# Reordering the last three steps of the FFN stages in a 10-stage transformer kernel on one Trainium2 core

## The chip, the cores and the metric

The kernel runs on one core of one Trainium2 chip, as one launch. The metric is the device time of one execution in microseconds (us). PE is the matmul engine (PEld its weight loads), DVE the vector engine, ACT the scalar engine, POOL the GpSimd engine, SP the engine that issues most DMAs here. Engines run apart from each other and meet at semaphores, which the kernel sets and waits for by hand.

## What is computed

Four transformer layers over 256 tokens of width 1024, in float32. In the reference, each FFN of the first two layers, and each of the last two, is

```python
def conv_ffn(h, w_in, conv_w, conv_b, w_out):
    z = causal_dwconv(h @ w_in, conv_w, conv_b)
    u, g = jnp.split(z, 2, axis=-1)
    return (jax.nn.gelu(g) * u) @ w_out
...
    h = rms_norm_2(x, g_ffn)
    a = depthwise_conv(h @ w_ffn_gate, conv_w, conv_b)
    x = x + (jax.nn.gelu(a) * (h @ w_ffn_up)) @ w_ffn_down

    e = rms_norm_2(pe @ w_ple_proj, g_ple)
    g = jax.nn.sigmoid(rms_norm_2(x, g_ple_in) @ w_ple_gate)
    return x + g * e
```

with D_FF = 2816. The last three lines are a gated embedding that follows each of the last two FFNs. The other stages are a pooling and attention mixer, a recurrent mixer, and two hybrid mixers with three attentions each. One of these attentions subtracts two softmaxes with a weight `lam` per layer, which is made of exponentials of two dot products of length 64.

## The kernel before

**Stages.** The ten stages are `pa`, `ffn0`, `rg`, `ffn1`, `hy0`, `hf0`, `ple0`, `hy1`, `hf1`, `ple1`. `ffn0` and `ffn1` are the causal FFNs, in which both halves of the first product go through a convolution. `hf0` and `hf1` are the others, in which only the gate half does. Activations live transposed, with the feature on the partition: x, h and so on are 8 tiles of 128 x 256 tokens.

**Weights as units.** All weights lie in HBM as 239 units of 128 x 2048 float32 (1 MB), in the order in which they are used. SP loads unit n into one of two `raw` slots once unit n - 2 has been taken from it (semaphore `lo_done`, in a loop of two loads at L359 to L363). ACT then rounds the unit to fp32r, `w_hi` (L385), and DVE takes the rest, `w_lo` (L794). There are three slots of these, so ACT waits until PE has finished unit n - 3 (`w_used`). In the code of both engines the call `after(n)` stands for this work on unit n + 3, and its place in the instruction order is set by hand.

**Products.** Each product is three matmuls (`three`, L1350 to L1352): hi by hi, hi by lo, lo by hi. Every unit of an FFN is 48 matmuls of 256 columns. The activations have such parts too: `h_hi` and `h_lo` for the normed input, `y_hi` and `y_lo` for the product that goes into the second matmul. ACT writes `y_hi` (L471), POOL writes `y_lo` (L1283, semaphore `ffy`).

**An FFN stage** has 11 steps of 256 features. Step s has two first products, a(s) into PSUM bank 4 and b(s) into bank 5, and then comes the second product of the step before, out(s-1), which adds to banks 0 to 3. So PE's order is a0 b0, a1 b1 out0, a2 b2 out1, ..., a10 b10 out9, out10, which are units 0 to 32 of the stage. In a causal stage, step s goes on like this after its products: DVE scales bank 4 by the row norm (L847), ACT makes the first tap (L446), and DVE adds the other two taps (L875; then semaphore `cvu`). The same happens for bank 5 (L456, L875; then `cvg`). ACT then takes the gelu (L461), DVE multiplies (L915; `ymul`), and ACT and POOL write `y_hi` and `y_lo`. In `hf` stages only bank 4 has taps, and the multiplication reads bank 5 directly. PE may write a(s+1) when the taps of bank 4 are done, and b(s+1) when those of bank 5 (or the multiplication) are done. There is one slot for y. Thus ACT writes `y_hi` of step s only when out(s-1) has been read by PE:

```python
                    act.wait_ge(sems["ymul"], done(1))
                    if s0:
                        act.wait_ge(sems["w_used"], plus(u + 3, i, 6))
                    nc.scalar.activation(pair(y_hi[:, 0], 0), pair(qk, 3), ACT.Copy).then_inc(sems["yhi"], 1)
```

Steps 3 to 8 are a hardware loop of two steps; 0 to 2, 9 and 10 are written out. In steps for which `parts_late` holds (all of `hf`, and step 10 of the causal stages) ACT and DVE do the work on later units behind, and not ahead of, the taps. The second slot of y, `y_hi[:, 1]`, holds the parts of the embedding through an `hf` stage. Its product (`ple`, `onto`) follows out10 directly.

**Between stages.** When a bank of out10 is complete, DVE adds it to x (L858), ACT and DVE write the parts of the next h, ACT squares x (L411), DVE sums the squares, and PE sums over the partitions (L1394). In `hy`, DVE also computes `lam` (L1163 to L1170) with an exponential on ACT (L680), once per layer, and ahead of `hy0` it works out position tables (`geometry`, L1115).

Of the kernel before, what the change touches and what calls it, by code (L numbers as in the profile page):

```python
# [21 lines left out]
ALU = mybir.AluOpType  # L22
# [20 lines left out]
LOOPED = 6  # L43
RG_STEPS = 5
# [40 lines left out]
def build(nc, W, XT, CON, CON0, VEC, PW, RW, PE_T, POSR, POSC, LAM, OUT, stages=STAGES):  # L85
# [4 lines left out]
    with ExitStack() as ctx:  # L90
# [22 lines left out]
        y_lo = sb("y_lo", [P, 2, 2, S], F32R)  # L113
        con = sb("con", [P, con_w])
# [8 lines left out]
        hr_t = sb("hr_t", [P, S])  # L123
        hr = hr_t[0:16, :]
# [10 lines left out]
        posr = sb("posr", [P, S], I32)  # L135
# [208 lines left out]
        @block.sync  # L344
        def _(sp):

            sp.dma_start(vec[:], VEC).then_inc(sems["vec_in"], 16)
            sp.dma_start(x[:], XT).then_inc(sems["x_in"], 16)
            sp.dma_start(raw[:, 0], W[first]).then_inc(raw_in[0], 16)
            sp.dma_start(con[:], CON).then_inc(sems["con_in"], 16)  # L350
            sp.dma_start(raw[:, 1], W[first + 1]).then_inc(raw_in[1], 16)
            sp.dma_start(posr[:], POSR.broadcast_to([P, S]))\
              .then_inc(sems["pos_in"], 16)
            sp.dma_start(posc[:], POSC).then_inc(sems["pos_in"], 16)
            sp.dma_start(lamv[:], LAM.broadcast_to([P, 8 * 64])).then_inc(sems["pos_in"], 16)
# [19 lines left out]
        def _(act):  # L375
# [44 lines left out]
            def ffn(s):  # L420
# [13 lines left out]
                def step(s0, i=None):  # L434
                    u = ub + (3 * s0 - 1 if s0 else 0)
# [29 lines left out]
                    if s0 and not late:  # L465
# [205 lines left out]
            def hy(s):  # L671
# [7 lines left out]
                act.wait_ge(sems["lam_exp"], 2 * L + 1)  # L679
                nc.scalar.activation(lamt[:, 2:4], lamt[:, 0:2], ACT.Exp).then_inc(sems["lam_exp"], 1)  # L680
# [84 lines left out]
            def hf_(s):  # L765
# [5 lines left out]
                nc.scalar.activation(y_hi[:, 1].rearrange("p a n -> p (a n)"), val[:, 0:512], ACT.Copy).then_inc(sems["pehi"], 1)  # L771
# [14 lines left out]
        def _(dve):  # L786
# [74 lines left out]
            def ffn(s):  # L861
# [17 lines left out]
                def step(s0, i=None):  # L879
                    u = ub + (3 * s0 - 1 if s0 else 0)  # L880
# [37 lines left out]
                    if s0:  # L918
# [52 lines left out]
            def outputs(s, g):  # L971
# [24 lines left out]
                link(V.tensor_scalar(rec[:, 1], rec[:, 1], lamt[:, 4:5], None, ALU.mult))  # L996
# [118 lines left out]
            def geometry():  # L1115
# [3 lines left out]
                V.tensor_copy(posf, posr[:])  # L1119
# [34 lines left out]
            def hy(s):  # L1154
# [6 lines left out]
                for j in range(2):  # L1161
                    o = (int(c) * 4 + 2 * j) * 64
                    link(V.tensor_tensor(lamp[:, j], lamv[:, o:o + 64], lamv[:, o + 64:o + 128], ALU.mult))  # L1163
                V.tensor_reduce(lamt[:, 0:2], lamp, AX.X, ALU.add).then_inc(sems["lam_exp"], 1)
# [3 lines left out]
                dve.wait_ge(sems["lam_exp"], 2 * L + 2)  # L1168
                link(V.tensor_tensor(lamt[:, 4:5], lamt[:, 2:3], lamt[:, 3:4], ALU.subtract))
                link(V.tensor_scalar(lamt[:, 4:5], lamt[:, 4:5], LAM0[int(c)], None, ALU.add))  # L1170
# [106 lines left out]
        def _(pool):  # L1277
# [7 lines left out]
            def ffn(s):  # L1285
                f = ffs.index(s)
                with pool.Fori(0, FF_STEPS) as i:
                    pool.wait_ge(sems["yhi"], i + (FF_STEPS * f + 1))
                    low(pair(y_lo[:, 0], 0), pair(qk, 3), pair(y_hi[:, 0], 0)).then_inc(sems["ffy"], 1)

# [25 lines left out]
            for s in used:  # L1316
# [27 lines left out]
        def _(pe):  # L1344
# [77 lines left out]
            def ffn(s):  # L1422
                f, ub, causal = ffs.index(s), B[s], kind(s) == "ffn"

                def step(s0, i=None):
                    u = ub + (3 * s0 - 1 if s0 else 0)
# [17 lines left out]
                    if s0:  # L1444
# [10 lines left out]
                pe.wait_ge(sems["ffy"], FF_STEPS * (f + 1))  # L1455
                onto(s, 0, ub + 32, y_parts(0), False, True)
# [498 lines left out]
```

## Time and profile before

| | us |
|---|---|
| median of 3 runs | 1805.56 |
| their range | 1802.94 to 1806.68 |
| the profiled execution | 1805.76 |
| its span, first to last instruction | 1803.9 |
| PE busy in the span | 1661.8 (92%) |
| DVE / ACT / POOL busy | 1134.5 / 919.2 / 163.3 |
| mean granted TensorE clock, of full speed | 0.953 |

### The profile page before, as it was taken

The numbers are of one execution on the slowest core, as the hardware profiler recorded it, in microseconds if no ns is written. First come the engines' busy times: TensorE is split into PE (matmuls) and PEld (weight loads), VectorE is DVE, ScalarE is ACT, GpSimd is POOL, SyncE is SP. The second block draws the span as 40 slices with busy tenths as digits, with TensorE's granted clock in tenths as the row PEclk, the third lists the DMA queues.
The fourth block names the chain that finished last, engine by engine and source line by source line (L and its number), as shares of the span: only waits on it lengthen the run. The fifth ranks groups of instructions, "written<-read, shape, count | busy, mean of one in ns | idle before, by whom it ended". The sixth has DMA issues, their size and how long they took to land.

```text
span 1803.9 us, 31136 instructions
## 1 busy us (share of the span) xinstructions
PE 1661.8 (92%) x12848; PEld 1583.4 (88%) x12848; DVE 1134.5 (63%) x1362; ACT 919.2 (51%) x1225; POOL 163.3 (9%) x98
## 2 busy tenths in 40 slices
PE   6889999798799989988999999998998999899997
PEld 6779999788799989867889999988967889899997
DVE  5428767777677676557536765676555644666656
ACT  5336455677555555525553544455434645454444
POOL 0030111000011110000013100000000002110000
PEclk9879999899899999979999999999988999999999
DMA  7214555444255544312224455544421223455451
GB/s 275 98 58 155 188 184 186 169 140 141 94 187 186 185 142 161 128 63 83 96 81 162 170 184 189 186 142 140 163 94 56 93 87 118 168 187 187 166 191 63
DMA packets 36251, 259.26 MB, mean 144 GB/s; under 512 B 4144, under 2 KB 4272, under 8 KB 5040
## 3 DMA queue, kind: packets, MB, share of 16 engines
q1 hardware_dynamic: 35712, 255.86, 41.2%
q8 instruction: 84, 1.38, 0.3%
q10 hardware_dynamic: 432, 1.84, 0.3%
q14 instruction: 23, 0.19, 0.0%
HBM read 256.63 MB, written 1.05 MB: 143 GB/s over the span
## 4 chain that ended last, share of the span: by engine, by line
PE 42%; issue 37%; DVE 10%; ACT 8%; DMA 1%; POOL 1%; POOLq 0%; SPq 0%; ACTq 0%; DVEq 0%
PE bank L1350 11%; PE bank L1352 10%; PE bank L1351 10%; ACT w_hi L385 3%; DVE w_lo L794 3%; PE bank L1521 3%; PE bank L1559 2%; PE bank L1501 2%; PE bank L1540 1%; DMA raw<-W 1%; ACT lg L554 1%; PE bank L1485 1%; POOL h_lo L1283 1%; DVE bank L847 1%; POOL y_lo L1283 1%
## 5 line engine op out<-in xcount | busy, mean ns | idle before, releaser
L1350 PE MATMUL bank<-h_hi,w_hi 128*128 128x256 f32 x2640 | 764.0, 289 | 40.3 <-DVE w_lo L794 15.7
L794 DVE TENSOR_TENSOR w_lo<-raw,w_hi 128x2048 fp32r<-128x2048 f32 x239 | 552.4, 2311 | 329.5 <-ACT w_hi L385 328.7
L1351 PE MATMUL bank<-h_lo,w_hi 128*128 128x256 f32 x2640 | 753.3, 285 | 0.0
L1352 PE MATMUL bank<-h_hi,w_lo 128*128 128x256 f32 x2640 | 752.6, 285 | 0.0
L385 ACT ACTIVATE w_hi<-raw 128x2048 fp32r<-128x2048 f32 x239 | 456.7, 1911 | 375.9 <-PE bank L1352 344.9
L1350 PEld LDWEIGHTS bank<-h_hi,w_hi 128*128 128x128 f32 x2640 | 513.3, 194 | 56.2 <-issue 32.5
L1351 PEld LDWEIGHTS bank<-h_lo,w_hi 128*128 128x128 f32 x2640 | 513.7, 195 | 0.4
L1352 PEld LDWEIGHTS bank<-h_hi,w_lo 128*128 128x128 f32 x2640 | 512.9, 194 | 0.0
L1350 PE MATMUL bank<-y_hi,w_hi 128*128 128x256 f32 x1040 | 299.1, 288 | 27.8 <-POOL y_lo L1283 27.1
L1352 PE MATMUL bank<-y_hi,w_lo 128*128 128x256 f32 x1040 | 296.9, 285 | 0.0
L1351 PE MATMUL bank<-y_lo,w_hi 128*128 128x256 f32 x1040 | 295.1, 284 | 0.0
L1350 PEld LDWEIGHTS bank<-y_hi,w_hi 128*128 128x128 f32 x1040 | 201.7, 194 | 32.5 <-POOL y_lo L1283 29.8
L1351 PEld LDWEIGHTS bank<-y_lo,w_hi 128*128 128x128 f32 x1040 | 201.6, 194 | 0.0
L1352 PEld LDWEIGHTS bank<-y_hi,w_lo 128*128 128x128 f32 x1040 | 200.9, 193 | 0.0
L1283 POOL TENSOR_TENSOR y_lo<-qk,y_hi 128x512 fp32r<-128x512 f32 x53 | 107.3, 2024 | 809.8 <-ACT y_hi L471 674.6
L847 DVE TENSOR_TENSOR bank<-bank,rinv_t 128x512 f32<-128x512 f32 x154 | 106.4, 692 | 103.8 <-PE bank L1352 103.2
L875 DVE SCALAR_TENSOR_TENSOR qk<-bank,vec,qk 128x255 f32<-128x255 f32 (+1 forms) x264 | 115.0, 477 | 41.1 <-ACT qk L446 32.7
L446 ACT ACTIVATE qk<-bank,vec 128x256 f32<-128x256 f32 x88 | 44.6, 557 | 94.3 <-DVE bank L847 94.3
L1559 PE MATMUL bank<-val,pt 128*128 128x64 f32 (+1 forms) x448 | 64.3, 290 | 21.4 <-ACT pt L533 21.4
L1559 PEld LDWEIGHTS bank<-val,pt 128*128 128x128 f32 x448 | 58.9, 204 | 26.4 <-ACT pt L533 23.9
L554 ACT ACTIVATE lg<-lg,nm 128x256 f32<-128x256 f32 x80 | 39.8, 498 | 66.6 <-DVE nm L963 66.5
L471 ACT ACTIVATE y_hi<-qk 128x512 fp32r<-128x512 f32 x44 | 27.4, 624 | 76.4 <-PE bank L1352 74.8
(203 smaller groups left out, 1390.1 us busy)
## 6 DMA issues: line engine op xcount, KB each, us to landing
raw<-W SPq DMA_DIRECT2D x239, 1024.0 KB, 4.8
wide<-RW ACTq DMA_DIRECT2D x1, 1280.0 KB, 5.4
con<-CON SPq DMA_DIRECT2D x1, 1258.0 KB, 10.5
x<-XT SPq DMA_DIRECT2D x1, 1024.0 KB, 5.6
OUT<-x SPq DMA_DIRECT2D x1, 1024.0 KB, 3.9
wide<-CON SPq DMA_DIRECT2D x1, 768.0 KB, 14.9
val<-PE_T ACTq DMA_DIRECT2D x2, 256.0 KB, 4.8
vec<-VEC SPq DMA_DIRECT2D x1, 394.0 KB, 3.0
```

The lines of the kernel that those rows point to most:

```text
L385: nc.scalar.activation(w_hi[:, n0 % NW], raw[:, n0 % NRAW], ACT.Copy).then_inc(sems["hi_done"], 1)
L446: ins = nc.scalar.activation(T[:, t], bank[4][:, t * S:(t + 1) * S], ACT.Identity, bias=b, scale=w)
L554: last = nc.scalar.activation(p, src, ACT.Exp, bias=nm[:, i, qt:qt + 1], scale=sc, accum_out=sums[:, m["col"], qt:qt + 1])
L794: V.tensor_tensor(w_lo[:, n0 % NW], raw[:, n0 % NRAW], w_hi[:, n0 % NW].bitcast(F32), ALU.subtract)\
L847: return V.tensor_tensor(z, z, rinv.unsqueeze(1).broadcast_to([P, w // S, S]), ALU.mult)\
L875: return V.scalar_tensor_tensor(out=dst, in0=src, scalar=w, in1=dst, op0=ALU.mult, op1=ALU.add)
L1283: return G.tensor_tensor(dst, src, hi.bitcast(F32), ALU.subtract)
L1350: T.matmul(out, w[0], a[0], start=start, stop=False, **kw)
L1351: T.matmul(out, w[0], a[1], start=False, stop=False, **kw)
L1352: return T.matmul(out, w[1], a[0], start=False, stop=stop, **kw)
L1521: last = T.matmul(b[:, qt * S:(qt + 1) * S], qk[p:p + w, tq, qt * P:(qt + 1) * P], qk[p:p + w, tk], start=a == 0, stop=a == n - 1)
L1559: last = T.matmul(o, pt[:, i % 2, kt * S + qt * P:kt * S + qt * P + P], value(m["v"], kt), start=kt == 0, stop=kt == 1)
```

## The change

Three things change.

**The last three steps of each FFN.** PE's order at the end of the stage becomes a9 b9, a10 b10, out8, out9, out10. The units are loaded in this order (`stored` maps position to unit), and SP's loop of loads is written out, 237 loads with fixed addresses. Step 9 uses the second slot of y, for which ACT does not wait for `w_used`, and step 10 the first again, after out8. ACT and DVE drop the work on a later unit from the end of step 9, and since step 10's positions are one lower (`u`), each later unit is prepared one place later in their order: position 31 in step 10 instead of at the end of step 9, and so on.

**The embedding's parts** get tensors of their own, `pe_hi` and `pe_lo`. To make room, `hr`, `posr` and `lamv` lose theirs and lie in `crs`, `geo` and `wide`. Since `posr` now lies in `geo`, DVE waits for its copy before it writes there.

**`lam`** of both layers is computed in `hy0`, with one product of 4 x 64 in place of two of 64, one reduction and one exponential of 4 values. `hy1` has none of it any more.

```diff
+FF_LAST = (29, 30, 28)
...
+        def stored(n):
+            for a in ffs:
+                u = n - B[a]
+                if 28 <= u <= 30:
+                    return first + B[a] + FF_LAST[u - 28]
+            return first + n
...
+        def y_slot(step):
+            return 1 if step == FF_STEPS - 2 else 0
...
-            with sp.Fori(0, N_UNITS // 2 - 1) as i:
-                for j in range(2):
-                    sp.wait_ge(sems["lo_done"], i * 2 + (j + 1))
-                    sp.dma_start(raw[:, j], W[bass.ds(i * 2 + (first + 2 + j), 1)].rearrange("a p n -> p (a n)"))\
-                      .then_inc(raw_in[j], 16)
...
+            for n in range(2, N_UNITS):
+                sp.wait_ge(sems["lo_done"], n - 1)
+                sp.dma_start(raw[:, n % NRAW], W[stored(n)]).then_inc(raw_in[n % NRAW], 16)
...
-                    u = ub + (3 * s0 - 1 if s0 else 0)
+                    u = ub + (3 * s0 - 1 if s0 else 0) - (s0 == FF_STEPS - 1)
...
                     act.wait_ge(sems["ymul"], done(1))
-                    if s0:
+                    if s0 and s0 != FF_STEPS - 2:
                         act.wait_ge(sems["w_used"], plus(u + 3, i, 6))
-                    nc.scalar.activation(pair(y_hi[:, 0], 0), pair(qk, 3), ACT.Copy).then_inc(sems["yhi"], 1)
-                    if s0 and late:
+                    nc.scalar.activation(pair(y_hi[:, y_slot(s0)], 0), pair(qk, 3), ACT.Copy).then_inc(sems["yhi"], 1)
+                    if s0 and late and s0 != FF_STEPS - 2:
                         after(u + 2, i)
...
-                    if s0:
+                    if s0 and s0 != FF_STEPS - 2:
                         after(u + 2, i)
...
-                act.wait_ge(sems["lam_exp"], 2 * L + 1)
-                nc.scalar.activation(lamt[:, 2:4], lamt[:, 0:2], ACT.Exp).then_inc(sems["lam_exp"], 1)
+                if L == 0:
+                    act.wait_ge(sems["lam_exp"], 1)
+                    nc.scalar.activation(lamt[:, 4:8], lamt[:, 0:4], ACT.Exp).then_inc(sems["lam_exp"], 1)
...
-                V.tensor_copy(posf, posr[:])
+                link(V.tensor_copy(posf, posr))
...
-                    if s0:
+                    if s0 and s0 < FF_STEPS - 2:
                         pe.wait_ge(sems["ffy"], done(0))
                         onto(s, 0, u + 2, y_parts(0), s0 == 1, False, i)
...
-                pe.wait_ge(sems["ffy"], FF_STEPS * (f + 1))
-                onto(s, 0, ub + 32, y_parts(0), False, True)
+                for s0 in range(FF_STEPS - 3, FF_STEPS):
+                    pe.wait_ge(sems["ffy"], FF_STEPS * f + s0 + 1)
+                    onto(s, 0, ub + 22 + s0, y_parts(y_slot(s0)), False, s0 == FF_STEPS - 1)
```

Instruction order on ACT in `ffn0`, steps 9 (from its gelu) and 10, before (the names are result<-operands, and `raw_in` says that a unit has landed):

```order
L461 ACTIVATE qk<-qk 128x512 [waits cvg]
L385 ACTIVATE w_hi<-raw 128x2048 [waits w_used,raw_in1]
L471 ACTIVATE y_hi<-qk 128x512 [waits w_used,ymul]
L446 ACTIVATE qk<-bank,vec 128x256 [waits scaled,ymul]
L446 ACTIVATE qk<-bank,vec 128x256
L385 ACTIVATE w_hi<-raw 128x2048 [waits w_used,raw_in0]
L456 ACTIVATE qk<-bank,vec 128x256 [waits scaled]
L456 ACTIVATE qk<-bank,vec 128x256
L461 ACTIVATE qk<-qk 128x512 [waits cvg]
L385 ACTIVATE w_hi<-raw 128x2048 [waits w_used,raw_in1]
L471 ACTIVATE y_hi<-qk 128x512 [waits w_used,ymul]
L385 ACTIVATE w_hi<-raw 128x2048 [waits w_used,raw_in0]
```

And the same place now:

```order
L472 ACTIVATE qk<-qk 128x512 [waits cvg]
L483 ACTIVATE y_hi<-qk 128x512 [waits ymul]
L457 ACTIVATE qk<-bank,vec 128x256 [waits scaled,ymul]
L457 ACTIVATE qk<-bank,vec 128x256
L396 ACTIVATE w_hi<-raw 128x2048 [waits w_used,raw_in1]
L467 ACTIVATE qk<-bank,vec 128x256 [waits scaled]
L467 ACTIVATE qk<-bank,vec 128x256
L472 ACTIVATE qk<-qk 128x512 [waits cvg]
L396 ACTIVATE w_hi<-raw 128x2048 [waits w_used,raw_in0]
L483 ACTIVATE y_hi<-qk 128x512 [waits w_used,ymul]
L396 ACTIVATE w_hi<-raw 128x2048 [waits w_used,raw_in1]
```

Step 9's `w_hi` between gelu and `y_hi` is gone, and step 9's `y_hi` no longer waits for `w_used`. The three others stand where they stood, each for a position one lower.

PE in `ffn0` at the end of b9, before:

```order
L1352 MATMUL bank<-h_hi,w_lo 128x256
L1350 MATMUL bank<-y_hi,w_hi 128x256 [waits lo_done,ffy]
L1351 MATMUL bank<-y_lo,w_hi 128x256
L1352 MATMUL bank<-y_hi,w_lo 128x256
L1350 MATMUL bank<-y_hi,w_hi 128x256
```

and now:

```order
L1371 MATMUL bank<-h_hi,w_lo 128x256
L1369 MATMUL bank<-h_hi,w_hi 128x256 [waits cvu,lo_done]
L1370 MATMUL bank<-h_lo,w_hi 128x256
L1371 MATMUL bank<-h_hi,w_lo 128x256
L1369 MATMUL bank<-h_hi,w_hi 128x256
```

Out8, which waited for `ffy` only, gave way to a10, which waits for the taps of bank 4 of step 9.

## Rows read from the trace of the kernel before

**Rows 1.** View of waits, PE: us in total, times, longest.

```profile
PE bank L1350 <- POOL y_lo L1283: 27.1, 8, 12.2
```

**Rows 2.** Timeline of PE, ends of the FFN stages: start, length, line [idle before <-releaser].

```profile
332.04 0.58 PE L1350 MATMUL bank<-y_hi,w_hi 128*128 128x256 f32 x1 [4.01 <-POOL y_lo L1283]
...
340.10 0.28 PE L1350 MATMUL bank<-h_hi,w_hi 128*128 128x256 f32 x1
...
660.38 0.39 PE L1350 MATMUL bank<-y_hi,w_hi 128*128 128x256 f32 x1 [4.01 <-POOL y_lo L1283]
...
667.65 0.28 PE L1350 MATMUL bank<-h_hi,w_hi 128*128 128x256 f32 x1
...
1188.82 0.39 PE L1350 MATMUL bank<-y_hi,w_hi 128*128 128x256 f32 x1 [2.13 <-POOL y_lo L1283]
...
1200.23 1.10 PE L1394 MATMUL bank<-sq,con 128*128 128x256 f32 x4
...
1753.36 0.39 PE L1350 MATMUL bank<-y_hi,w_hi 128*128 128x256 f32 x1 [2.13 <-POOL y_lo L1283]
...
1766.21 1.03 PE L1394 MATMUL bank<-sq,con 128*128 128x256 f32 x4
```

**Rows 3.** Busy time by stretch: last three columns are PEclk, DMA share, GB/s.

```profile
334.00:336.00 2.00, 2.00 (x11) 2.00 (x11) 0.82 (x2) 0.27 (x1) 0.00 (x0) 0.50 1.20 356
```

**Rows 4.** Timeline of DVE, ACT and POOL, step 10 of ffn0.

```profile
316.65 0.70 DVE L847 TENSOR_TENSOR bank<-bank,rinv_t 128x512 f32<-128x512 f32 x1 [0.62 <-PE bank L1352]
...
326.77 0.69 DVE L915 TENSOR_TENSOR qk<-qk 128x512 f32<-128x512 f32 x1 [0.70 <-ACT qk L461]
...
328.45 0.61 ACT L471 ACTIVATE y_hi<-qk 128x512 fp32r<-128x512 f32 x1
...
329.14 2.85 POOL L1283 TENSOR_TENSOR y_lo<-qk,y_hi 128x512 fp32r<-128x512 f32 x1 [11.96 <-ACT y_hi L471]
```

**Rows 5.** Timeline of DVE and PE, step 9 of ffn0.

```profile
303.69 1.77 DVE L875 SCALAR_TENSOR_TENSOR qk<-bank,vec,qk 128x255 f32<-128x255 f32 x4
...
305.04 0.28 PE L1350 MATMUL bank<-y_hi,w_hi 128*128 128x256 f32 x1
...
309.46 1.77 DVE L875 SCALAR_TENSOR_TENSOR qk<-bank,vec,qk 128x255 f32<-128x255 f32 x4
...
311.93 0.69 DVE L915 TENSOR_TENSOR qk<-qk 128x512 f32<-128x512 f32 x1 [0.70 <-ACT qk L461]
```

**Rows 6.** Timeline of PE, start of a1 in ffn0.

```profile
155.13 0.35 PE L1350 MATMUL bank<-h_hi,w_hi 128*128 128x256 f32 x1 [1.47 <-DVE qk L875]
```

**Rows 7.** Timeline of hf0, steps 9 and 10: DVE, PE, ACT, POOL.

```profile
1159.98 1.78 DVE L875 SCALAR_TENSOR_TENSOR qk<-bank,vec,qk 128x255 f32<-128x255 f32 x4 [1.15 <-ACT qk L446]
...
1163.69 0.28 PE L1350 MATMUL bank<-y_hi,w_hi 128*128 128x256 f32 x1
...
1164.82 0.69 DVE L915 TENSOR_TENSOR qk<-qk,bank 128x512 f32<-128x512 f32 x1
...
1186.78 0.63 ACT L471 ACTIVATE y_hi<-qk 128x512 fp32r<-128x512 f32 x1 [3.73 <-PE bank L1352]
...
1187.48 1.28 POOL L1283 TENSOR_TENSOR y_lo<-qk,y_hi 128x512 fp32r<-128x512 f32 x1 [15.87 <-ACT y_hi L471]
```

**Rows 8.** Timeline of ACT and PE, second unit of hy1.

```profile
1249.95 0.20 ACT L680 ACTIVATE lamt<-lamt 128x2 f32<-128x2 f32 x1 [1.97 <-DVE lamt L1164]
...
1253.07 0.36 PE L1350 MATMUL bank<-h_hi,w_hi 128*128 128x256 f32 x1 [1.04 <-ACT sq L497]
```

**Rows 9.** Line L363 of SP, the weight loads in the loop: ns (DMA: us) min/median/max.

```profile
L363 SPq FUSED_REGOPS  x236: 46/46/52, 15.7 to 1756.1; - x118
...
DMA to landing us min/median/max: 4.7/4.8/7.2
```

**Rows 10.** The page's costliest groups: busy us, mean ns of one | idle before.

```profile
L794 DVE TENSOR_TENSOR w_lo<-raw,w_hi 128x2048 fp32r<-128x2048 f32 x239 | 552.4, 2311 | 329.5 <-ACT w_hi L385 328.7
...
L385 ACT ACTIVATE w_hi<-raw 128x2048 fp32r<-128x2048 f32 x239 | 456.7, 1911 | 375.9 <-PE bank L1352 344.9
```

More of the change, by code:

```diff
@@ L134, in build @@
         odr = sb("odr", [P, 4, 2])
-        posr = sb("posr", [P, S], I32)
+        posr = geo[:, 3].bitcast(I32)
         posc = sb("posc", [P, 2], I32)
@@ L464, in step @@
                         after(u + 1, i)
-                    if s0 and not late:
+                    if s0 and not late and s0 != FF_STEPS - 2:
                         after(u + 2, i)
                     act.wait_ge(sems["ymul"], done(1))
-                    if s0:
+                    if s0 and s0 != FF_STEPS - 2:
                         act.wait_ge(sems["w_used"], plus(u + 3, i, 6))
-                    nc.scalar.activation(pair(y_hi[:, 0], 0), pair(qk, 3), ACT.Copy).then_inc(sems["yhi"], 1)
-                    if s0 and late:
+                    nc.scalar.activation(pair(y_hi[:, y_slot(s0)], 0), pair(qk, 3), ACT.Copy).then_inc(sems["yhi"], 1)
+                    if s0 and late and s0 != FF_STEPS - 2:
                         after(u + 2, i)
@@ L770, in hf_ @@
                 act.wait_ge(sems["pe_in"], 16 * (ffs_hf.index(s) + 1))
-                nc.scalar.activation(y_hi[:, 1].rearrange("p a n -> p (a n)"), val[:, 0:512], ACT.Copy).then_inc(sems["pehi"], 1)
+                nc.scalar.activation(pe_hi[:], val[:, 0:512], ACT.Copy).then_inc(sems["pehi"], 1)
                 ffn(s)
@@ L1159, in hy @@
                 scale_group(s, 0)
[L1161 to L1164, printed above, removed]
+                if L == 0:
+                    z = lamv.rearrange("p (a b n) -> p a b n", a=4, b=2)
+                    link(V.tensor_tensor(lamp, z[:, :, 0], z[:, :, 1], ALU.mult))
+                    V.tensor_reduce(lamt[:, 0:4], lamp, AX.X, ALU.add).then_inc(sems["lam_exp"], 1)
                 V.tensor_scalar(nsink[:], v_(f"sink{c}", 0, 8), -1.0, None, ALU.mult)
@@ L1167, in hy @@
                     cosines()
-                dve.wait_ge(sems["lam_exp"], 2 * L + 2)
-                link(V.tensor_tensor(lamt[:, 4:5], lamt[:, 2:3], lamt[:, 3:4], ALU.subtract))
-                link(V.tensor_scalar(lamt[:, 4:5], lamt[:, 4:5], LAM0[int(c)], None, ALU.add))
+                    dve.wait_ge(sems["lam_exp"], 2)
+                    for a in range(2):
+                        link(V.tensor_tensor(lamt[:, 8 + a:9 + a], lamt[:, 4 + 2 * a:5 + 2 * a], lamt[:, 5 + 2 * a:6 + 2 * a],
+                                             ALU.subtract))
+                        link(V.tensor_scalar(lamt[:, 8 + a:9 + a], lamt[:, 8 + a:9 + a], LAM0[a], None, ALU.add))
                 after(ub)
@@ L1286, in ffn @@
                 f = ffs.index(s)
-                with pool.Fori(0, FF_STEPS) as i:
+                with pool.Fori(0, FF_STEPS - 2) as i:
                     pool.wait_ge(sems["yhi"], i + (FF_STEPS * f + 1))
                     low(pair(y_lo[:, 0], 0), pair(qk, 3), pair(y_hi[:, 0], 0)).then_inc(sems["ffy"], 1)
+                for s0 in (FF_STEPS - 2, FF_STEPS - 1):
+                    a = y_slot(s0)
+                    pool.wait_ge(sems["yhi"], FF_STEPS * f + s0 + 1)
+                    low(pair(y_lo[:, a], 0), pair(qk, 3), pair(y_hi[:, a], 0)).then_inc(sems["ffy"], 1)
             def to_h(s, src):
@@ L1323, in _ @@
                         pool.wait_ge(sems["pehi"], ffs_hf.index(s) + 1)
-                        low(y_lo[:, 1].rearrange("p a n -> p (a n)"), val[:, 0:512], y_hi[:, 1].rearrange("p a n -> p (a n)"))\
-                            .then_inc(sems["pe_ready"], 1)
+                        low(pe_lo[:], val[:, 0:512], pe_hi[:]).then_inc(sems["pe_ready"], 1)
                     ffn(s)
@@ L1748, in ple @@
                 pe.wait_ge(sems["pe_ready"], L + 1)
-                onto(s, 0, ub, y_parts(1), True, True)
+                onto(s, 0, ub, [(pe_hi[:, k * S:(k + 1) * S], pe_lo[:, k * S:(k + 1) * S]) for k in range(2)], True, True)
                 normed(s)
```

24 lines of the change are left out of this document (11 added, 13 removed).

## The prediction

> **What bounds the kernel now.** I read the page first: PE is busy 92% of the span, so time is to be had only where PE stands still or runs at the lower clock. The view of waits for PE says for what it stands still; its largest entry is POOL's `y_lo`, 27.1 us in 8 waits [rows 1]. One of them, 12.2 us, ends the `rg` stage, which the change leaves alone. The timeline of PE then shows where the others are: in front of out10, the last product of each FFN stage [rows 2]. The reader is to see four brackets there, 4.01, 4.01, 2.13 and 2.13 us, and after each the start of the next kind of product, from which the length of the last products follows. From the timeline of the other engines comes why: with one slot for y, ACT may write `y_hi` of step 10 only once out9 has been read, and POOL's `y_lo` comes behind it. In `hf0` these are 0.63 and 1.28 us, all of it after out9 [rows 7]. In `ffn0` ACT also had a `w_hi` ahead of it, and `y_lo` took 2.85 us [rows 4].
>
> **What a normal unit takes.** In `hf0` two units of second products run from 1188.82 to 1200.23, which is 11.41 us at full clock, or 5.70 us for one [rows 2]. All units of an FFN have 48 matmuls of this size, so I use 5.70 for each.
>
> **The waits that go.** A bracket is 0.16 us shorter than the delay, as matmuls overlap. So the delays are 4.17 + 4.17 + 2.29 + 2.29 = 12.92 us.
>
> **The clock behind them.** Out10 of `ffn0` takes 340.10 - 332.04 = 8.06 us, 2.36 more than a normal unit; the granted clock in that stretch is 0.50, that is 1.2 GHz [rows 2, 3]. PE had stood still for 4 us before. In `ffn1` it is 667.65 - 660.38 = 7.27, so 1.57 more. In `hf1` two units take 1766.21 - 1753.36 = 12.85, so 1.44 more, and in `hf0` nothing, after the same 2.13 us of idle time. The sum is 5.37 us. I take all of it as regained, since PE no longer stops there. The bounds are 5.37 and nothing.
>
> **Is the cover long enough?** Once a10 and b10 are done, two units (out8 and out9) now cover the path of y10 where out9 alone did. In the causal stages I follow `ffn0`. Step 9's elementwise work keeps its times up to its multiplication, which ends at 311.93 + 0.69 = 312.62 [rows 5]. Before, DVE could begin step 10 (the scaling of bank 4) right when a10 ended; now a10 ends before that multiplication does, so step 10 begins at 312.62. From that scaling to the end of `y_lo` it took 329.14 + 2.85 - 316.65 = 15.34 us [rows 4]; it ends at 327.96. PE's side: a10 starts at 305.51 (below), b10 at 311.28, and then three units of 5.70 end at 328.38, when out10 can start. So 0.42 us are left and there is no wait. What ended step 9's `y_hi` late before, `w_used`, is gone, and so is ACT's `w_hi` ahead of it. DVE makes the weight parts for position 32 after step 10's multiplication, which ends at 312.62 + 326.77 + 0.69 - 316.65 = 323.43 [rows 4], so they are there by 325.8, and those of the next stage by 330.3 even if they wait for `y_lo` at 2.31 us each [rows 10]. PE wants them at 328.38 and 334.1.
>
> In this trace `y_lo` takes 2.85 us in `ffn0`, where DVE's `w_lo` runs beside it, and 1.28 us in `hf0`, where DVE is idle at that time [rows 4, 7]. The Trainium skill (page "SBUF — State Buffer", section "SBUF: two separate sides") says that DVE and GpSimd share a port pair under an exclusive lock, held for a whole instruction. By that rule the worst case is a `y_lo` behind a whole `w_lo`, 2.31 + 1.28 = 3.59 us by rows 10 and 7, 0.74 longer, so that out10 would wait 0.3 us in each causal stage and the sum would be 0.6 us smaller. I keep the 2.85, because the same `w_lo` starts just ahead of it in the new order too.
>
> In the `hf` stages y10 needs out8's end, 5.70 us before out9's. From the start of `y_hi` to the end of `y_lo` it is 1187.48 + 1.28 - 1186.78 = 1.98 us, so 3.7 us are left [rows 7].
>
> **The waits that come.** a10 and b10 now each have one unit where they had two between them and the taps. In `ffn0` the taps of bank 4 are done at 303.69 + 1.77 = 305.46, and b9 gives way at 305.04 [rows 5]. With the 0.05 us that lie between the end of `y_lo` and the start of PE [rows 2, 4] a10 starts at 305.51, 0.47 late. b10 could start at 311.21, and its taps end at 309.46 + 1.77 = 311.23, so it is 0.07 late. That is 0.54 us a stage, 1.1 for two. The nearest row for such a spacing without an out product between is the start of a1, 1.47 us idle, 1.63 late [rows 6]; it stands behind the stage's norm as well, so I take the row of step 9 and keep 1.63 for each of a10 and b10 as the upper bound. In `hf0` the taps end at 1161.76, ahead of b9's end at 1163.69, and the multiplication that frees bank 5 ends at 1165.51, while a10 runs until 1169.4 [rows 7]. Nothing is lost there.
>
> **`lam`.** In `hy1` ACT stood still for 1.97 us before its exponential, and the evacuation of bank 0 came behind that and a `w_hi`; PE then waited 1.04 us for this evacuation, 1.20 late [rows 8]. Without the exponential ACT is some 3 us earlier, so I count 1.2 us. The bounds are nothing and 1.2. In `hy0` the values of both layers are made at once; the few larger operands lie beside products. The added wait behind `posr` is one handover, 0.05 us, on the path into `hy0`; I take 0.1.
>
> **SP.** The register step of 46 ns in front of each load goes [rows 9]. Were it on the path at each of 236 loads, that would be 10.9 us, but in FFN stages no load is waited for. I take nothing. The separate tensors for the embedding cost nothing: the same copies at the same places in the order.
>
> **The sum.** 12.92 + 5.37 - 1.1 + 1.2 - 0.1 = 18.3 us. The profiled execution took 1805.76, of which 1803.9 are the span; it lies 0.2 above the median of the runs. I predict 1787.5.
>
> **Rivals.**
> - *The clock's time does not come back.* PE stops at many other places, and the 2.13 us of `hf0` cost nothing while those of `hf1` cost 1.44 [rows 2]. So where the lower clock falls is partly chance. If what is saved at these four places falls elsewhere, the gain is 12.9, and the time is 1792.9. Against it speaks that nothing new stops PE there for more than 0.5 us. The Trainium skill ("TensorE: Matmul & The Clock Gate", section "Part 1: The HAM clock gate") says that the monitor behind the clock runs freely and is not tied to the kernel's start. By this rule the 5.4 us are a draw of one run; the four unequal rows agree.
> - *The step-9 spacing is dearer.* If a10 and b10 each start 1.63 late in the causal stages, as a1 did, this costs 3.26 in place of 0.54 a stage: 1793.0. For it: DVE and ACT have two steps' work closer together. Against it: the times of step 9 in rows 5.
> - *The last wait stays, so that the change does not do what it says in the causal stages.* The margin is 0.42 us. If step 10's work slips by one `w_lo` of 2.31 us, out10 waits 1.9 us twice: 1791.3.
> - *Slower: the loads.* SP's loads are written out with fixed addresses, and each raw slot goes round by a load, a `w_hi` and a `w_lo` while PE does two units, 11.40 us. Now this is 4.8 + 1.91 + 2.31 = 9.02 [rows 9, 10]. From a load of 7.18 us on, the loads are the bound, and from 7.33 on (0.15 x 239 / 2 = 18 us) the kernel is slower than before. At 7.4 us a load the time is 1813.8. For it speaks only that a load of 7.2 us occurs in this trace. Against it: bytes, layout and queue are the same.
>
> **Chances.** Forecast 0.70; clock 0.14; spacing 0.07; last wait 0.07; loads 0.02. The range goes up to the first two rivals, and down by the runs' own spread (2.6 below the median) and by the 1.1 and some register steps that I may have charged wrongly: 1783 to 1793.5. A measurement of this kernel can tell 0.2%, 3.6 us, from no change, so faster means below 1802. All but the last rival are faster; with something left for several small losses together: faster 0.95, same 0.03, slower 0.02.
>
> **What the new profile would show.** Right: no bracket of over 0.5 us in front of the out products at the ends of FFN stages, out10 of 5.7 us each, brackets of about 0.3 with the taps (the DVE line that was L875) in front of a10, and none at the second unit of `hy1`. PE's waits for `y_lo` fall from 27.1 to about 15. Wrong: `y_lo` still in front of out10, taps of over 1 us in front of a10 or b10, a mean clock that is not above 0.953, or loads of over 7 us.

## The result, and the profile after

| | us |
|---|---|
| before, median of 5 runs beside it | 1805.56 (1802.94 to 1807.31) |
| after, median of 5 runs | 1794.8 (1789.83 to 1795.53) |
| ratio, with 95% interval | 0.9931 [0.9915, 0.9946] |
| the profiled execution after | 1795.39, its span 1793.6 |
| PE / DVE / ACT / POOL busy in it | 1654.8 / 1134.1 / 917.2 / 163.5 |
| mean granted clock in it | 0.955 |

The change makes the kernel 0.7% faster. By the ratio that is 1805.56 x (1 - 0.9931) = 12.5 us, and 10.4 us between the two profiled executions. The forecast was 18.3. Two repetitions (e5 and e10 below) gave 0.5% and 0.6%. Two executions that ran far longer than all others, 8184 us in e1 and 2515 us in e3, are left out of the medians below.

I read the profile after in the order of the prediction. The waits of PE first (us in total, times, longest):

```profile
PE bank L1369 <- DVE w_lo L807: 16.9, 2, 15.4
PE bank L1666 <- DVE qk L1083: 14.9, 5, 8.4
PE bank L1369 <- DVE h_lo L822: 14.7, 4, 11.2
PE bank L1369 <- POOL y_lo L1299: 14.6, 4, 12.2
```

`y_lo` fell from 27.1 us in 8 waits [rows 1] to 14.6 in 4, as forecast. But a wait for `h_lo` has grown to 11.2 us. Its longest was 6.3 us before, as this row of the timeline of PE before shows:

```profile
1235.98 0.55 PE L1350 MATMUL bank<-h_hi,w_hi 128*128 128x256 f32 x1 [6.29 <-DVE h_lo L809]
```

**The ends of the FFN stages.** The timeline of PE after, in `ffn0`: the start of a10, of out8, and of the first product of the next stage.

```profile
307.81 0.36 PE L1369 MATMUL bank<-h_hi,w_hi 128*128 128x256 f32 x1 [0.42 <-DVE qk L888]
...
319.39 0.28 PE L1369 MATMUL bank<-y_hi,w_hi 128*128 128x256 f32 x1
...
336.35 0.28 PE L1369 MATMUL bank<-h_hi,w_hi 128*128 128x256 f32 x1
```

Between 319.39 and 336.35 no row has a bracket. Three units in 16.96 us are 5.65 us each, where out10 alone took 8.06 [rows 2]. In `ffn1` it is the same:

```profile
644.34 0.28 PE L1369 MATMUL bank<-y_hi,w_hi 128*128 128x256 f32 x1
...
661.31 0.28 PE L1369 MATMUL bank<-h_hi,w_hi 128*128 128x256 f32 x1
```

The busy time by stretch (PE, PEld, DVE, ACT, POOL, granted clock, DMA share, GB/s) has 1.00 where it had 0.50 [rows 3]:

```profile
334.00:336.00 2.00, 2.00 (x19) 2.00 (x18) 2.00 (x5) 1.05 (x3) 0.00 (x0) 1.00 0.91 381
```

The other engines, step 10 of `ffn0`, which answer to [rows 4]:

```profile
324.83 0.69 DVE L928 TENSOR_TENSOR qk<-qk 128x512 f32<-128x512 f32 x1 [0.70 <-ACT qk L472]
326.64 5.59 DVE L807 TENSOR_TENSOR w_lo<-raw,w_hi 128x2048 fp32r<-128x2048 f32 x2 [1.12 <-ACT w_hi L396]
...
326.51 0.61 ACT L483 ACTIVATE y_hi<-qk 128x512 fp32r<-128x512 f32 x1
...
315.55 1.30 POOL L1299 TENSOR_TENSOR y_lo<-qk,y_hi 128x512 fp32r<-128x512 f32 x1 [13.29 <-ACT y_hi L483]
327.20 2.88 POOL L1299 TENSOR_TENSOR y_lo<-qk,y_hi 128x512 fp32r<-128x512 f32 x1 [10.36 <-ACT y_hi L483]
```

`y_lo` of step 10 ends at 330.08, and out10 starts two units behind out8, at about 330.7. So the cover was just long enough.

**The profile by stage.** I cut the timeline of PE at the start of each stage's norm product (L1394 before, L1413 after). A part ends with the norm of the next stage, so the end of an FFN lies in the part that ends at the next norm. In us, one profiled execution each:

| part | before | after | gain |
|---|---|---|---|
| start | 23.34 | 23.82 | -0.48 |
| `pa` to `ffn0` | 123.44 | 125.15 | -1.71 |
| `ffn0` to `rg` | 199.07 | 193.14 | 5.93 |
| `rg` to `ffn1` | 129.87 | 132.40 | -2.53 |
| `ffn1` to `hy0` | 202.31 | 197.31 | 5.00 |
| `hy0` to `hf0` | 328.27 | 326.26 | 2.01 |
| `hf0` to `ple0` | 193.93 | 191.53 | 2.40 |
| `ple0` to `hy1` | 44.13 | 49.22 | -5.09 |
| `hy1` to `hf1` | 326.48 | 324.94 | 1.54 |
| `hf1` to `ple1` | 195.37 | 191.51 | 3.86 |
| `ple1` to end | 37.69 | 38.32 | -0.63 |

The four FFN parts gained 17.2 us. The others lost 6.9 on balance: 5.1 in `ple0`, 2.5 in `rg`, and the rest in small pieces of both signs.

**Where `ple0` lost it.** The timeline of ACT after, at the start of `ple0` (norm product at 1189.61):

```profile
1200.71 1.91 ACT L396 ACTIVATE w_hi<-raw 128x2048 fp32r<-128x2048 f32 x1 [3.57 <-DMA raw<-W]
...
1204.60 1.92 ACT L396 ACTIVATE w_hi<-raw 128x2048 fp32r<-128x2048 f32 x1 [1.61 <-DMA raw<-W]
...
1209.98 1.92 ACT L396 ACTIVATE w_hi<-raw 128x2048 fp32r<-128x2048 f32 x1 [3.46 <-DMA raw<-W]
...
1218.46 1.91 ACT L396 ACTIVATE w_hi<-raw 128x2048 fp32r<-128x2048 f32 x1 [6.56 <-DMA raw<-W]
```

Before, the same stretch (norm product at 1200.23) has no wait for a load. ACT waits for PE there, which is the normal case:

```profile
1212.52 1.92 ACT L385 ACTIVATE w_hi<-raw 128x2048 fp32r<-128x2048 f32 x1 [3.87 <-PE bank L1352]
1218.28 1.92 ACT L385 ACTIVATE w_hi<-raw 128x2048 fp32r<-128x2048 f32 x1 [3.84 <-PE bank L1352]
1224.04 1.92 ACT L385 ACTIVATE w_hi<-raw 128x2048 fp32r<-128x2048 f32 x1 [3.84 <-PE bank L1352]
```

The last of these stands ahead of the exponential's table on ACT, and its `w_lo` ahead of the scaling of the gate's first bank on DVE. After:

```profile
1220.40 2.29 DVE L807 TENSOR_TENSOR w_lo<-raw,w_hi 128x2048 fp32r<-128x2048 f32 x1 [5.90 <-ACT w_hi L396]
1222.61 1.29 DVE L860 TENSOR_TENSOR bank<-bank,rinv_t 128x512 f32<-128x512 f32 x2
```

The last `w_hi` starts 1224.04 - 1200.23 = 23.81 us behind the norm before, and 1218.46 - 1189.61 = 28.85 after. The 5.04 us between the two reach `x`, then `h_lo`, and then PE at the start of `hy1`:

```profile
1230.40 0.55 PE L1369 MATMUL bank<-h_hi,w_hi 128*128 128x256 f32 x1 [11.16 <-DVE h_lo L822]
```

The cause stands in the order of the instructions. Before, ACT and DVE ended step 10 with `after` of positions 29, 30 and 31, which are the units 32, 33 and 34, and 34 is the second unit of the next stage. Since `u` is one lower in step 10 now, they end with 31, 32 and 33. Unit 34 comes behind the next norm. Until its `w_lo` is done its raw slot is taken, so the load of unit 36, which goes into the same slot, is issued later too.

**In `rg`** the same thing shows as a bracket in front of the second unit, where before PE went on without one. The timeline of PE after:

```profile
344.55 0.36 PE L1369 MATMUL bank<-h_hi,w_hi 128*128 128x256 f32 x1 [1.42 <-DVE w_lo L807]
...
358.89 3.35 PE L1666 MATMUL bank<-qk,wide 128*128 128x256 f32 x7 [8.36 <-DVE qk L1083]
```

The second bracket was 6.39 us before. Over the whole span the line of the loads shows who waits for them:

```profile
L378 SPq DMA_DIRECT2D raw<-W x237: 327/328/328, 15.4 to 1763.8; - x119
...
  ACT w_hi L396: 56.8, 19
...
DMA to landing us min/median/max: 4.7/4.9/7.1
```

Before it was 31.0 us in 11 waits. The loads themselves take what they took [rows 9]: they are issued later, not slower.

### The profile page after: what moved, and what is told of

It is laid out like the page before. It is cut to its first block, busy times and chain, and to the rows that moved or that the text cites. A ratio compares the mean times of both kernels' runs of the same rounds, so it can differ in the third digit from the quotient of the medians.

```text
span 1793.6 us, 30271 instructions
## 1 busy us (share of the span) xinstructions
PE 1654.8 (92%) x12848; PEld 1576.8 (88%) x12848; DVE 1134.1 (63%) x1358; ACT 917.2 (51%) x1222; POOL 163.5 (9%) x98
## 4 chain that ended last, share of the span: by engine, by line
PE 70%; DVE 13%; ACT 10%; issue 4%; DMA 2%; POOL 0%; ACTq 0%; SPq 0%; DVEq 0%; POOLq 0%
PE bank L1369 21%; PE bank L1371 20%; PE bank L1370 20%; DVE w_lo L807 4%; ACT w_hi L396 4%; PE bank L1541 3%; DMA raw<-W 2%; PE bank L1579 2%; PE bank L1521 2%; PE bank L1560 1%; DVE x L871 1%; ACT lg L566 1%; ACT sq L422 1%; DVE h_lo L822 1%; DVE bank L860 1%
## 5 line engine op out<-in xcount | busy, mean ns | idle before, releaser
L1369 PE MATMUL bank<-y_hi,w_hi 128*128 128x256 f32 x1008 | 286.8, 285 | 15.4 <-POOL y_lo L1299 14.6
L1371 PE MATMUL bank<-y_hi,w_lo 128*128 128x256 f32 x1008 | 284.9, 283 | 0.0
L1370 PE MATMUL bank<-y_lo,w_hi 128*128 128x256 f32 x1008 | 283.2, 281 | 0.0
L1369 PEld LDWEIGHTS bank<-y_hi,w_hi 128*128 128x128 f32 x1008 | 192.4, 191 | 19.5 <-POOL y_lo L1299 16.8
L1370 PEld LDWEIGHTS bank<-y_lo,w_hi 128*128 128x128 f32 x1008 | 192.2, 191 | 0.0
L1371 PEld LDWEIGHTS bank<-y_hi,w_lo 128*128 128x128 f32 x1008 | 191.8, 190 | 0.0
```

The source lines that it names most:

```text
L1369: T.matmul(out, w[0], a[0], start=start, stop=False, **kw)
L1370: T.matmul(out, w[0], a[1], start=False, stop=False, **kw)
L1371: return T.matmul(out, w[1], a[0], start=False, stop=stop, **kw)
```

## The experiments

The theory: the 17.2 us that were forecast for the FFN ends came, and some 8 were given back because each stage behind an FFN is entered with one unit less prepared. The rivals: the given-back time is scatter of the clock, or it belongs to another part of the change (`lam`, the tensors, SP). The column "parts" below is cut as in the table above, and `u` is that of the change. Runs come in three jobs, each with runs of before beside them, and each ratio is to those: e1 to e4 (median of before 1803.44), e5 to e8 (1805.84), and e9 and e10, on another chip (1804.52).

**e3: before, with the last preparation of step 10 left out.** If the theory holds, this alone makes `rg` and `ple0` as long as they are after the change.

```diff
 # before.py, ACT
-                    if s0 and late:
+                    if s0 and late and s0 != FF_STEPS - 1:
                         after(u + 2, i)
 # DVE
-                    if s0:
+                    if s0 and s0 != FF_STEPS - 1:
                         after(u + 2, i)
```

> The kernel before, without the last preparation of step 10 in each FFN stage (it is made behind the next norm, as in the changed kernel). Theory A: the loss alone, about 2.5 us in rg and 5 us in ple0, 1811 to 1814 against 1805.6, less what DVE gains at the FFN ends by having no w_lo there (up to 1 us a stage). Theory B: 1804 to 1807.

Measured: 1814.19 us, ratio 1.0057 [1.0037, 1.0078]. `rg` took 133.51 (129.87 before), `ple0` 49.07 (44.13), `ple1` 38.36 (37.69). The FFN parts stayed: 199.14, 202.32, 193.80 and 195.35. The timeline of PE has the two brackets of the change, in a kernel that has nothing else of it:

```profile
345.25 0.36 PE L1350 MATMUL bank<-h_hi,w_hi 128*128 128x256 f32 x1 [1.41 <-DVE w_lo L794]
...
359.57 2.93 PE L1646 MATMUL bank<-qk,wide 128*128 128x256 f32 x6 [8.34 <-DVE qk L1070]
...
1245.80 0.55 PE L1350 MATMUL bank<-h_hi,w_hi 128*128 128x256 f32 x1 [12.11 <-DVE h_lo L809]
```

So the later preparation is enough to cause the losses in `rg`, `ple0` and `ple1`. `hy0` took 331.56 here (328.27 before), but that part varies by as much from one execution to the next.

**e4: the change without the reordering.** `lam`, the tensors and SP's written-out loop stay. The order is the old one, with one slot for y. The lines shown are a part of the edit; the others put back the old places of the preparations.

```diff
-FF_LAST = (29, 30, 28)
+FF_LAST = (28, 29, 30)
...
-            return 1 if step == FF_STEPS - 2 else 0
+            return 0
...
-                    u = ub + (3 * s0 - 1 if s0 else 0) - (s0 == FF_STEPS - 1)
+                    u = ub + (3 * s0 - 1 if s0 else 0)
...
-                for s0 in range(FF_STEPS - 3, FF_STEPS):
+                for s0 in range(FF_STEPS - 1, FF_STEPS):
```

> The changed kernel with the reordering undone: one y slot, the old order of units, everything else of the change (lam once, written-out loads, own tensors for the embedding's parts). By the sum of the prediction: 1.2 us less than before through lam in hy1, 0.1 more through geometry, loads and tensors nothing: about 1804.4, the four waits of 4.01, 4.01, 2.13 and 2.13 us in place. If the written-out loads are slower, or the shared tensors bring a wait, it lies above 1806, and some of the 10.8 us belongs to that.

Measured: 1803.29 us, ratio 0.9988 [0.9975, 1.0001]. `rg` 129.52 and `ple0` 44.12 are as before, and the four FFN parts sum to 790.73, against 790.68 before. So the gain at the FFN ends and the loss in `rg` and `ple0` belong to the reordering. Of the single FFN parts, `ffn0` is 0.8 us shorter and `ffn1` 0.8 longer than before (198.29 and 203.14); the last section comes back to that. What `lam` gives, 1.2 us by the forecast, agrees with the ratio (2.2 us, between nothing and 4.5), but isn't told apart from nothing by it.

**e8: e4 with the second slot for step 10.** Step 10's y goes into the second slot and doesn't wait for `w_used`, in the old order.

```diff
-            return 0
+            return 1 if step == FF_STEPS - 1 else 0
...
-                    if s0:
+                    if s0 and s0 != FF_STEPS - 1:
                         act.wait_ge(sems["w_used"], plus(u + 3, i, 6))
```

> The old order of units and preparations, but y of step 10 goes into the second slot and its y_hi does not wait for out9. Theory: in hf stages the second slot is all that is needed (y_hi and y_lo are done some 2 us before out9 ends): the waits of 2.13 us go, hf0's part 191.5 or up to 1.5 more where w_lo now meets the additions to x, ple0's 44.1. In the causal stages y_hi stood behind a w_hi anyway, so 4.01 us stay nearly whole, 3.9 or so. Ratio to before about 0.996. Rival (the reordering is needed everywhere): all four waits stay.

Measured: 1802.88 us, ratio 0.9991 [0.9972, 1.001]. The gain is smaller than I expected (0.996). The causal waits stand where they stood, and those of the `hf` stages are gone:

```profile
333.12 0.58 PE L1369 MATMUL bank<-y_hi,w_hi 128*128 128x256 f32 x1 [4.01 <-POOL y_lo L1299]
...
661.09 0.39 PE L1369 MATMUL bank<-y_hi,w_hi 128*128 128x256 f32 x1 [4.01 <-POOL y_lo L1299]
```

In the causal stages not the slot but the work of step 10 itself is longer than one unit of products, so the slot alone gives nothing there, and it takes the order. In `hf0` and `hf1` the parts are 193.37 and 193.39, still 1.9 longer than after the change, where I had allowed for 1.5. In the timeline of DVE a `w_lo` of 2.29 us now stands ahead of the additions to x. The rival, that the reordering is needed everywhere, holds for the causal stages; in `hf` the slot alone takes the wait away, but gives only a part of the time.

**e1 and e2: the change with unit 34 prepared at the end of step 10 again.** In e1 on both engines; in e2 on ACT, while on DVE its `w_lo` comes behind the first addition to x.

```diff
 # e1, ACT and DVE, at the end of each step
+                    if s0 == FF_STEPS - 1:
+                        after(u + 3, i)
 # e2, DVE instead, in the update of x by bank b
+                    if kind(s) in ("ffn", "hf") and b == 0:
+                        after(B[s] + 31)
```

> The changed kernel, with one more preparation (w_hi on ACT, w_lo on DVE, for the second unit of the next stage) at the end of step 10 of each FFN stage, as before the change. Theory A (the change enters each next stage with one unit less prepared, which cost 2.5 us in rg and 5.1 us in ple0): rg's part, from the norm matmul of rg to that of ffn1, falls from 132.4 to about 130, ple0's (to that of hy1) from 49.2 to about 44.5; DVE's w_lo now stands ahead of the first addition to x, which may cost up to 1.5 us a stage; median 1787 to 1791. Theory B (the loss is chance of the clock, or SP's written-out loads are slower): rg and ple0 stay at 132 and 49, median 1794 to 1796 or more.

> As the run before, but DVE's w_lo of that unit stands behind its first addition to x. Theory A: rg's and ple0's parts fall as there, and the FFN's end pays less for it, under 1 us a stage; median 1786 to 1790. Theory B: 1794 to 1796.

Measured: e1 1805.77 us, ratio 1.001 [0.9991, 1.0028]; e2 1800.63, ratio 0.998 [0.996, 1.0]. Both miss what I expected by 10 us and more. They repair `rg` (128.90 and 128.96) and `ple0` (44.71 and 44.16), though not `ple1`, which grew to 39.83 and 39.69. But they lose more at the ends of the causal stages: `ffn0` takes 200.83 and 200.34, `ffn1` 202.57 and 201.68, against 193.14 and 197.31 after the change. The timeline of ACT in e2 says why:

```profile
334.05 1.92 ACT L396 ACTIVATE w_hi<-raw 128x2048 fp32r<-128x2048 f32 x1 [5.85 <-DMA raw<-W]
...
335.87 0.89 ACT L417 ACTIVATE h_hi<-x,vec 128x256 fp32r<-128x256 f32 x2
```

and in PE's timeline of the same kernel what follows:

```profile
339.82 0.36 PE L1373 MATMUL bank<-h_hi,w_hi 128*128 128x256 f32 x1 [4.06 <-DVE h_lo L824]
```

Unit 34 has not landed yet. ACT stands still for the load, and `h_hi`, which PE wants, is queued behind it. The load is late because unit 32, whose raw slot it needs, is prepared one place later in step 10 than before. The first of the three loads in each of these rows is that of unit 34, before and in e2:

```profile
322.78 11.87 SPq L363 DMA_DIRECT2D raw<-W  x3
...
328.22 10.42 SPq L378 DMA_DIRECT2D raw<-W  x3
```

And before, this is where ACT prepared it, with no bracket:

```profile
328.97 1.90 ACT L385 ACTIVATE w_hi<-raw 128x2048 fp32r<-128x2048 f32 x1
```

That is inside the 4.01 us in which PE stood still for `y_lo`, up to 332.04 [rows 2]. So the wait that the change removed had covered something: a part of the preparation of the next stage.

**e6 and e9: the preparation restored for `hf0` alone.** There `ple0` is next, where the loss is largest, and one unit of products more lies ahead.

```diff
 # ACT, at the end of each step
+                    if s == "hf0" and s0 == FF_STEPS - 1:
+                        after(u + 3, i)
 # DVE, in the update of x by bank b
+                    if s == "hf0" and b == 0:
+                        after(B[s] + 31)
```

> The changed kernel with the one preparation more (w_hi behind step 10's last on ACT, w_lo behind DVE's first addition to x) in hf0 alone. Theory A (one unit less prepared costs 5.1 us in ple0; in the causal stages the same repair fails because the load has not landed): ple0's part falls from 49.2 to 44.2, hf0's rises from 191.5 to 192.3, all others as in the changed kernel; 4.3 us faster than it, a ratio to before of about 0.9905. Rival (the ends of the FFN stages pay in any case what ple0 gains): hf0 rises by 4 us or more, nothing gained.

Measured: 1788.4 us, ratio 0.9908 [0.9887, 0.9928], as expected. `hf0` takes 192.32 (0.8 more than after the change), `ple0` 44.17 (5.1 less). The bracket at the start of `hy1` is back at its size of before:

```profile
1226.21 0.55 PE L1373 MATMUL bank<-h_hi,w_hi 128*128 128x256 f32 x1 [6.29 <-DVE h_lo L824]
```

I ran it once more on another chip, with the change itself beside it.

> The change with unit hf0's successor prepared as before (the second unit's w_hi and w_lo of ple0's stretch made at the end of hf0 and in ple0's first update), once more, beside the change itself on the same chip. Theory (one unit less prepared at a stage's entry costs time where the next stretch is short): ple0 44.2 us and hf0 192.3 us in the profile, 3.8 us to 4.3 us less in those two stretches together than in the change, so a ratio to before lower than the change's by 0.002 to 0.003. Rival (the two are alike and the earlier difference was scatter of the clock): the same ratio within 0.001.

Measured: 1790.97 us, ratio 0.9925 [0.9906, 0.9944]; `hf0` 192.31, `ple0` 43.05. The ratio is 0.0013 below that of e10, between what I expected (0.002 to 0.003) and the rival (within 0.001).

**e5 and e10: the change as it is, again.**

> The changed kernel itself, on the chip of the three runs beside it. Theory A and B: as measured first, a ratio to before of 0.993, give or take 0.0015; rg's part 132.4, ple0's 49.2, ffn0's 193.1, ffn1's 197.3.

> The change as it is, in the same job. Theory: ple0 49.2 us and hf0 191.5 us in the profile, ratio to before 0.993 to 0.995. Rival: the ratio of e9 within 0.001.

Measured: e5 1795.34 us, ratio 0.9952 [0.9935, 0.9969], a little above what I expected (0.9915 to 0.9945); e10 1794.81 us, ratio 0.9938 [0.9922, 0.9953]. The parts `hf0` 191.52 and 191.52, `ple0` 49.36 and 48.91 repeat those of the first profile. So in the profiles e6 and e9 save 3.9 to 5.5 us in `hf0` and `ple0` together. In the medians they were 6.9 us faster (e6 against e5) and 3.8 us (e9 against e10). The intervals of the ratios lie apart in the first job and overlap in the second, so the size of this gain is known from the parts better than from the times. It is the best version that I found, 0.1 to 0.4% below the change.

**e7: e6, and in `rg` the second unit's parts ahead of the squares.**

```diff
 # on top of e6, in the norm: ACT ahead of the squares, DVE ahead of their sum
+                if s == "rg":
+                    after(B[s] - 2)
```

> As the run before, and at the start of rg the preparation of its second unit stands ahead of the squares on ACT and of their sum on DVE instead of behind them. Theory A: the second unit's w_lo is ready by the time PE wants it, and the load behind it is issued some 2 us earlier, on which rg's chain of load, w_hi, w_lo and elementwise work hangs: rg's part falls from 132.4 to 130 to 131, and the norm's matmul comes up to 1.5 us later. Rival (rg hangs on its norm and not on the loads): rg's part stays or grows by 1.9 us, the length of the w_hi put ahead.

Measured: 1792.36 us, ratio 0.9929 [0.9912, 0.9947]. `rg` falls to 129.98, but `ffn0` grows to 195.44, since the norm product itself now waits 2.16 us for DVE's sum of the squares. The norm comes 2.3 us later, where I had allowed for 1.5. The two parts together take 325.42, against 325.54 after the change. The loss in `rg` moved and did not go.

**The FFN parts and the rest, over all profiles.** This table tells the change's gain and loss apart from the scatter:

| kernel | the four FFN parts | everything else |
|---|---|---|
| before | 790.68 | 1013.2 |
| e3 (before, one unit less prepared) | 790.61 | 1024.8 |
| e4 (no reordering) | 790.73 | 1011.5 |
| after, e5, e10 | 773.49, 773.48, 774.77 | 1020.1, 1016.7, 1021.0 |
| e6, e9 (unit 34 ready for `ple0`) | 774.26, 774.29 | 1012.3, 1010.0 |
| e7 (e6, and `rg`'s second unit ahead of the squares) | 776.6 | 1013.5 |
| e8 (second slot, old order) | 788.4 | 1007.1 |
| e1, e2 (unit 34 ready for all) | 790.2, 786.7 | 1005.8, 1010.6 |

## Why the prediction was right or wrong

It forecast 1787.5 us, in 1783.0 to 1793.5. The ratio puts the change at 0.9931 x 1805.56 = 1793.1, the upper end of the range, and the median of 1794.8 lies above it. The ratios of e5 and e10 would put it at 1796.9 and 1794.4. The sign was right, and so was about half (e5) to two thirds (the first ratio) of the gain. That the first ratio falls inside the range is luck: the range's upper end was set by two rivals (1792.9 and 1793.0) that did not happen, and the loss that did happen had no place in the sum.

- **The waits that go (12.92) and the clock behind them (5.37), less the waits that come (1.1).** Forecast 17.2 us, measured 17.2 (5.93 + 5.00 + 2.40 + 3.86), again 17.2 in e5, and 15.9 in e10. The units took 5.65 us where I had 5.70. I had given the clock's part as between nothing and 5.37; all of it came back. The rival by which it falls elsewhere (1792.9) comes close to the measured time, but is not what happened: e3 and e4, which keep the old order, have 790.61 and 790.73 us in the four FFN parts together, against 790.68 before, so the sum of what the lower clock costs at these four places is no draw of one run. The share of a single causal stage is: out10 took 8.06 us in `ffn0` and 7.27 in `ffn1` before, and 7.28 and 7.96 in e4, as PE's timeline there shows:

```profile
335.28 0.39 PE L1369 MATMUL bank<-y_hi,w_hi 128*128 128x256 f32 x1 [4.01 <-POOL y_lo L1299]
...
342.56 0.29 PE L1369 MATMUL bank<-h_hi,w_hi 128*128 128x256 f32 x1
...
662.49 0.58 PE L1369 MATMUL bank<-y_hi,w_hi 128*128 128x256 f32 x1 [4.01 <-POOL y_lo L1299]
...
670.45 0.28 PE L1369 MATMUL bank<-h_hi,w_hi 128*128 128x256 f32 x1
```

The Trainium skill ("TensorE: Matmul & The Clock Gate", section "Part 1: The HAM clock gate") has the monitor run freely. The causal stages agree: the same 4.01 us of idle time cost 1.6 us at one place and 2.3 to 2.4 at the other, and which of the two costs more differs between kernels. `hf0` and `hf1` show no such change (below).
- **The cover.** I had a10 0.47 late, and its bracket is 0.42, so 0.58 late by the rule of 0.16. With the 2.2 us by which this execution reaches `ffn0` later (0.48 + 1.71), my `y_lo` would end at 327.96 + 2.2 = 330.2. It ended at 330.08, and out10 had no wait. `y_lo` took 2.88 us, where I had kept 2.85 against the worst case of 3.59. So the rival of a last wait that stays (1791.3) fell, and so did that of a dearer spacing (1793.0).
- **`lam` (1.2).** The bracket of 1.04 us [rows 8] is gone. The part of `hy1` is 1.5 us shorter. But this part took 321.7 to 325.3 us in the profiles of kernels that all have this edit, so the size of what `lam` gives is not settled.
- **SP and the tensors (nothing).** Nothing is seen of them in e4. The rival of slower loads fell: 4.7, 4.9 and 7.1 us to landing, against 4.7, 4.8 and 7.2.
- **The step that failed** is that which reads "DVE makes the weight parts for position 32", "and those of the next stage by 330.3", and "PE wants them at 328.38 and 334.1". It looks at unit 33, the first of the next stage, and there it holds. It does not ask for the next one. The rows of orders ahead of the prediction show three `w_hi` in step 10 before and after, "each for a position one lower", and one at step 9 that goes. I put the moved ones at nothing without a reason and never said where the one that falls off the end is made up. It is unit 34, and it comes behind the norm of the next stage. That cost 2.5 us in `rg`, 5.1 in `ple0` and 0.6 in `ple1`: 8.2 us together, where the profile missed the forecast by 8.0. What is left, 1.7 us in `pa`, 0.5 at the start and a gain of 2.0 in `hy0`, is within what these parts do from one execution to the next (`pa` took 119.3 to 125.2 us in profiles of kernels with the same code there).
- Nor did I ask what the removed wait had covered. e1 and e2 show that it can't simply be put right: with the wait gone and unit 32 prepared one place later, the load of unit 34 lands too late for it to be prepared at the old place. Restored in `hf0` alone it gives about half of the 8.2 us back (3.9 to 5.5 in the parts).

Shown by runs: that the missing unit causes the loss (e3 adds it alone, e6 takes the largest piece back). Open: whether the loss in `rg` can be had back. Three placements of the work were tried there (e1, e2 and e7): each made `rg` shorter and `ffn0` longer by about as much or more. Two ways by which unit 34's load would land earlier weren't tried: a third raw slot, and unit 32's parts earlier in step 10. After the change ACT made that `w_hi` at 324.70, while PE was done with b10, whose slot it takes, at 319.39.

## What to carry to other kernels

When an order of products is changed, count for each engine what stands between two fixed points before and after, and name where each piece of look-ahead work that fell out is made up, past the end of the stage as well. Where a wait is removed, ask what was done during it: this one had hidden the preparation of the unit after next, and nearly half of the gain came back as waits in the stages behind. The short stage that can least afford it pays most: `ple0`, with few products and much elementwise work, paid 5.1 us, and the long `hy` stages nothing that stands clear of their own variation of some 5 us.

## What the runs showed of the hardware

- **The time of one kernel goes with the granted clock.** The twelve runs of e5 went from 1787.45 us at a mean clock of 0.961 to 1802.71 at 0.952. In the profiles of the change itself `hy0` took 326.26, 326.16 and 331.59 us, while `hf0` and `hf1` took 191.5 each time. So a part in which PE hardly stops mostly repeats to 0.1 us (`ffn0` was 1.3 us longer once, in e10), and one in which it stops often only to some 5 us.
- **The same idle time can cost clock in one place each time and never in another.** 2.13 us in front of out10 cost 1.44 us more behind it in `hf1` and nothing in `hf0` [rows 2]. The two parts were 193.93 and 195.37 before, 193.80 and 195.35 in e3, and 193.92 and 195.39 in e4. So here it is not chance, as I had put it, though these runs don't say what the difference is. In the causal stages the cost does change places, as said above.
- **DVE and POOL.** `y_lo` took 1.30 us where DVE was not in `w_lo` and 2.88 us beside it, and two `w_lo` took 5.59 us beside it against 4.50 without:

```profile
342.11 4.50 DVE L807 TENSOR_TENSOR w_lo<-raw,w_hi 128x2048 fp32r<-128x2048 f32 x2 [0.70 <-ACT w_hi L396]
```

The Trainium skill ("SBUF — State Buffer", section "SBUF: two separate sides") has the two share a port pair under an exclusive lock. The rows agree in size too, if the two `w_lo` are taken apart:

```profile
326.64 2.29 DVE L807 TENSOR_TENSOR w_lo<-raw,w_hi 128x2048 fp32r<-128x2048 f32 x1 [1.12 <-ACT w_hi L396]
...
328.97 3.27 DVE L807 TENSOR_TENSOR w_lo<-raw,w_hi 128x2048 fp32r<-128x2048 f32 x1
```

The first has its usual length, and `y_lo`, which starts at 327.20, ends at 330.08, 1.15 us behind the end of that `w_lo` at 328.93. The second starts while `y_lo` runs and ends 2.16 us behind it. So each waits for what is left of the other's instruction and then takes about its own time. The prediction's worst case of 3.59 us for `y_lo` would need both to start together; here `w_lo` had a lead of 0.56 us.
